# Dividing six PSUM banks between two kinds of work: three for the gates' products in place of two

## The reference, cut to what matters

```
p = h @ w_in;  xr, gate = split(p, [1536])          # 1536 = 12 heads x 128
xc = causal_depthwise_conv(xr, conv_w, conv_b)      # 4 taps
r = sigmoid(xh[head] @ w_rg[head] + b_rg)           # the gates' products: one 128x128
i = sigmoid(xh[head] @ w_ig[head] + b_ig)           # matrix per head and gate
a = exp(-8 * r * softplus(-lam))
hs = scan(a, sqrt(1 - a*a) * (i * xc))              # along time
y = hs * silu(gate)
h = h + y @ w_out
```

## Time and profile before

| | |
|---|---|
| median of 3 runs | 1717.25 us |
| the profiled execution's own time | 1717.2 us |
| its span, first to last instruction | 1715.1 us |
| PE busy | 1691.4 us, 99% |
| DVE, ACT, POOL busy | 871.1, 763.2, 967.1 us |
| mean granted TensorE clock | 0.999 |

### The profile page before, as it was taken

The page is one execution under the profiler, slowest core; times in us unless marked ns, Lnnn a source line. Parts: engine busy times, 40 slices in busy tenths (PEclk is TensorE's granted clock), DMA queues, the critical chain, the costliest instruction groups (busy, mean ns, idle before and its releaser), DMA issues.

```text
span 1715.1 us, 20931 instructions
## 1 busy us (share of the span) xinstructions
PE 1691.4 (99%) x8044; PEld 1396.4 (81%) x8044; DVE 871.1 (51%) x1251; ACT 763.2 (44%) x1203; POOL 967.1 (56%) x606
## 2 busy tenths in 40 slices
PE   9999999999999999999999999999999999999998
PEld 7888888777778997888888888888678888888887
DVE  4999997757787885522212121386644221212124
ACT  5223335377867763343222222454765332323234
POOL 5859655657678575654444444664547444444464
PEclk9999999999999999999999999999999999999999
DMA  5322323222245233222222222222112222222221
GB/s 177 100 97 87 123 98 112 98 73 87 86 183 201 68 124 130 99 96 92 95 98 98 99 98 99 86 98 99 50 48 89 98 99 98 99 92 94 97 99 62
DMA packets 56258, 172.65 MB, mean 101 GB/s; under 512 B 6496, under 2 KB 14816, under 8 KB 55264
## 3 DMA queue, kind: packets, MB, share of 16 engines
q1 hardware_dynamic: 56160, 171.33, 28.9%
HBM read 165.01 MB, written 6.29 MB: 100 GB/s over the span
## 4 chain that ended last, share of the span: by engine, by line
PE 70%; DVE 5%; ACT 3%; issue 2%; POOL 1%; DMA 1%; SPq 0%; DVEq 0%; ACTq 0%
PE B L319 57%; PE B L1712 1%; PE B L2464 1%; PE B L2466 1%; PE B L2462 1%; PE B L2260 1%; PE B L2360 1%; PE B L2339 1%; DVE SW L1175 1%; PE B L302 1%; DVE B L1041 1%; PE B L1639 1%; PE B L1604 1%; PE B L304 1%; PE B L303 1%
## 5 line engine op out<-in xcount | busy, mean ns | idle before, releaser
L295 POOL TENSOR_TENSOR WL<-RAW,WH 128x1024 fp32r<-128x1024 f32 x280 | 679.0, 2427 | 618.3 <-ACT WH L291 618.0
L291 ACT ACTIVATE WH<-RAW 128x1024 fp32r<-128x1024 f32 x281 | 296.8, 1058 | 634.3 <-PE B L319 600.2
L319 PE MATMUL B<-P0h,WH 128*128 128x512 f32 x1088 | 424.6, 390 | 2.0 <-DVE Yl L444 1.8
L319 PE MATMUL B<-P0l,WH 128*128 128x512 f32 x1088 | 418.0, 389 | 0.3 <-DVE P0l L448 0.3
L319 PE MATMUL B<-P0h,WL 128*128 128x512 f32 x1088 | 274.4, 389 | 0.0
L319 PEld LDWEIGHTS B<-P0h,WH 128*128 128x128 f32 x1088 | 204.3, 188 | 45.8 <-DVE Yl L444 2.6
L319 PEld LDWEIGHTS B<-P0l,WH 128*128 128x128 f32 x1088 | 204.3, 188 | 42.8 <-DVE P0l L448 0.8
L319 PEld LDWEIGHTS B<-P0h,WL 128*128 128x128 f32 x1088 | 204.2, 188 | 42.4
L455 DVE TENSOR_TENSOR H<-H,B 128x512 f32<-128x512 f32 x88 | 60.2, 686 | 288.2 <-PE B L319 288.1
L1992 DVE SCALAR_TENSOR_TENSOR TMP<-B,RS 128x512 f32<-128x512 f32 x64 | 44.1, 691 | 258.5 <-PE B L319 244.1
L319 PE MATMUL B<-P1h,WH 128*128 128x512 f32 x448 | 174.7, 390 | 0.0
(11 more groups left out here) (362 smaller groups left out, 2686.5 us busy)
## 6 DMA issues: line engine op xcount, KB each, us to landing
RAW<-in_w SPq DMA_DIRECT2D x281, 512.0 KB, 3.2
PX<-in_zeros SPq DMA_DIRECT2D x4, 1024.0 KB, 9.4
H<-in_xT SPq DMA_DIRECT2D x8, 256.0 KB, 5.4
U<-u SPq DMA_DIRECT2D x32, 64.0 KB, 2.0
g<-GB SPq DMA_DIRECT2D x8, 256.0 KB, 2.2
GB<-g SPq DMA_DIRECT2D x32, 64.0 KB, 2.0
out<-Q SPq DMA_DIRECT2D x4, 512.0 KB, 3.6
CA<-in_zeros SPq DMA_DIRECT2D x1, 1920.0 KB, 10.0
```

Source lines behind the costliest of these rows:

```text
L291: act.activation(WH[:, i % NS, :], RAW[:, i % NR, :], ACT.Copy).then_inc(*inc("w_hi", i))
L295: eng.tensor_tensor(WL[:, i % NS, :], RAW[:, i % NR, :], WH[:, i % NS, :].bitcast(F32), ALU.subtract).then_inc(*inc(lo_of(i), i))
L319: return pe.matmul(b[:, :], w[:, ws[c]], x[:, c, :], start=start, stop=stop)
```

## The change

One number: how many of the six banks go to `rbanks`. The gates' products go round in three banks in place of two; X and G go round in three in place of four. From O0 on all six are in one queue, as before.

```
     def pe_odd(pe):
-        for _ in range(2):
+        for _ in range(3):
             rbanks.queue.append(banks.queue.popleft())
```

## The result

The changed kernel takes 1737.41 us (median of 4 runs, 1736.43 to 1738.10) against 1717.61 (4 runs) before. The ratio is 1.0114, 95% interval 1.0103 to 1.0126: 19.8 us slower. The profiled execution took 1737.19 us, its span is 1735.1.

A forecast was written before the change was run, and what follows sets the result against it. TensorE, busy 99% of the span, was taken as the bound, so new waits are paid in full: 1717.2 + 11.95 (19.0 of new waits, less 2.1 swallowed and 4.95 won in rounds) + 2.2 for the clock = 1731.3 us, range 1727.5 to 1737.5.

The forecast's parts named there:

- The new waits: TensorE's units X3, X8, X10, G3, G9 and O2 wait for VectorE's low parts to free banks: 19.0 us in all.
- The rounds: Gates' products in R0, R1 and R2 lose less with three banks: 0.8, 3.1 and 1.05 us won, 4.95 in all.
- the forecast's own reason for R1: At R1 VectorE and ScalarE have caught up with a TensorE 6 us late, so stalls of 4.0 shrink to 0.9.
- faster rival: Only the gates' waits change, the banks' return does not bind: 4.95 us less, 1712.2 us; chance 0.04.
- Waits swallowed: Today's bank waits at X11 (0.6 us) and G10 (1.5 us) vanish behind the new waits: 2.1 us.
- The running delay: How much later TensorE is at a place than in the trace before; forecast 11.95 us after O2.
- The clock: One fall of TensorE's clock to half rate, in G9's 6.9 us wait: 2.2 us, the middle of none and 4.4.
- the three falls as a rival: The clock falls in all three long waits (X8, G3, G9), 2.2 us each: 1734 to 1736 us; chance 0.18.
- The rows at the span's end: Granted clock still 1.00 in the 5.2 us of TensorE's last four matmuls, 0.50 in the 1.8 us behind.
- X10's wait: X10 waits for X7's bank, 1.5 us; the three-falls rival let it swallow 1.5 us of the first fall.
- The range: 1727.5 to 1737.5 us: from 1729.1 less 1.6 for the sum's small terms, up to three falls.
- D: TensorE's running delay against the trace before; 11.9 us after O2, none of it given back to the kernel's end.

The follow-up runs named there:

- without the square root: The changed kernel with the recurrence's square root replaced by a second tanh, one table load of 1.28 us a round less: 1733.46 us, ratio 1.0091.
- The loss alone: Against the kernel before: X and G in three banks, gates' products still in two, sixth bank idle until O0: 1742.13 us, ratio 1.0146.
- The lent bank: The kernel before (two gates' banks, four for units), with the units' oldest bank lent to the gates for each round R: 1714.18 us, ratio 0.9982.
- the filled kernel: The changed kernel with 20, 16 and 29 matmuls on old data ahead of X8, G3 and G9, filling the long waits: 1732.90 us, ratio 1.0086.
- statistics' wait filled: The kernel before with one bank lent to the gates per round, plus four matmuls on old data between X0 and X1: 1713.96 us, ratio 0.9984.
- half filled: The changed kernel with 9, 7 and 14 matmuls on old data ahead of X8, G3 and G9: 1732.64 us, ratio 1.0092.

## Why the prediction was right, and where it was not

- **The new waits.** Forecast from start to start: X3 1.3, X8 4.9, X10 1.5, G3 3.8, G9 6.9, O2 0.6, sum 19.0. Measured: 1.3, 4.85, 1.6, 3.8, 6.9, 0.6, sum 19.0. The step that carried it, to ask of each low part what starts its chain and move it by that alone, was right at every place. The experiment without the square root shows it for X8 and G3. For G9 the same experiment shows its limit: the length of VectorE's table computations there is not fixed, and the forecast held because GpSimd's work lay beside them as before.
- **The rounds.** Forecast 4.95 us won, measured 23.7 - 18.1 = 5.6. The loss alone, set against the kernel before, shows that 2.0 of these come from TensorE's lateness at R1, as the forecast's own reason for R1 said. Its faster rival overlooked that: 1712.2 us counts R1's 3.1 us although TensorE would not be late there. The lent bank shows 3.1 us won in the rounds without lateness, and 1714.2 us. The seven waits of the earlier trace rows are not all that the rounds waited for banks: the 1.6 us of R1 stands under another entry (L302 <- DVE Yl L444: 1.8 us in 2), so the modelled tails are only a part of why the view shows less than the timeline. Waits swallowed: 2.1 both.
- **The running delay** without the clock's part at O3 is then 19.0 - 2.1 - 5.6 = 11.3 (and 0.2 for slower first matmuls behind waits), where 11.95 was forecast. In the filled kernel, where the first matmuls behind all six waits are slower and no unit is, it is 12.0.
- **The clock** is the term that was mis-sized: "I take the middle, 2.2 us, for one fall, in the 6.9 us wait". The size of a fall came out right (X8 2.4, G3 1.8, G9 2.3, from the units' lengths), their number did not. All three long waits brought one, 6.5 us (6.1 against the filled kernel's units), and the profiled execution had two more of 1.6 us each, in X1 and Q2. So the clock's term measured 9.7 us in that execution, where 2.2 was forecast: 7.5 us more. The rounds (0.6 more won) and the wait at L1728 (1.4, below) took a part of this back, and 5.7 us stand between the 14.1 forecast and the 19.8 measured. I had the three falls as a rival at 1734 to 1736 us and gave it 0.18. The rows at the span's end show a clock that stays up for 5.2 us with little work, but I read them as if the shorter waits were safe; they say nothing of another place. The size was luck in part. It is the middle between nothing and 4.4, and the earlier trace rows don't bound it from above: a matmul that is still slow at 8.89 says that the low level lasted at least until then.
- **X10's wait** did not swallow 1.5 us of the first fall, as that rival had it: it is 1.6 us in the changed kernel and 1.5 in the filled one. X7's low part comes behind the scaling of X8, which waits for X8's end, so a slower X8 moves the wait and doesn't fill it. The forecast had this dependence, and the rival left it out.
- **The range** held by 0.1 us, and that is luck. Its upper end was called three falls; the forecast's terms give 1735.7 for these, and the two more falls stood in no case.
- **What was given back.** I had D stay at its value to the end. In this trace some 21.4 us had come together behind Q2 (11.5, the clock's 9.7 and 0.2 from before X0), and 20.0 stood at the end. The wait at L1728 explains it, 2.4 us in the trace of before and 1.0 here. It is 0.9 to 2.3 in the other traces: 1.7 in the unchanged kernel's second one, 2.3 in the filled kernel, 0.9 in the lent one. So it doesn't go with the delay, and no run ties it to the change.

## What to carry to other kernels

Before a bank (or any buffer) is moved from one ring to another, list for each user of the smaller ring when its buffer came back and when the next one started, and add up what is short; ask what starts the chain that gives it back, since that tells by what it will move. When TensorE gets a new wait of well over 2 us, count a second price of about 2 us for the clock behind each, not behind the longest alone; with shorter ones it may come or not. And where two users are busy at different times, lend the buffer rather than divide it: here that turned 20 us of loss into 5 of gain.

## What the runs showed of the hardware

- The granted clock fell behind waits with 2.7, 3.3, 3.6, 4.7, 5.0 and 6.7 us of idle TensorE, and also behind 2.4 (G3 without the square root, whose unit took 1.6 us more than behind a wait at full clock). Shorter waits went both ways. It fell behind 2.1 us (filled, at 607) and 1.9 (statistics' wait filled, R1), and stayed up behind 2.1 (half filled, G3), 1.8 (lent, R1) and 1.6 (before, R1), one trace each. The price was 1.3 to 2.8 us a fall, by the unit behind it against the 5.57 us that it takes behind a wait at full clock.
- The clock falls by chance as well. Runs of the kernel before spread over 4.7 us in one group of 23 and 6.5 in another of 17, and the mean granted clock of a run goes with its time: in the group of 17 the kernel before took 1715.1 to 1716.3 us at 0.999 (5 runs), 1716.9 to 1718.0 at 0.998 (10) and 1720.0 and 1721.6 at 0.996.
- A VectorE operation on two tensors in SBUF (L1280 to L1283) takes 0.68 us alone and 1.6 to 2.9 beside operations of GpSimd (L295 and L1118). L444 or L1046, which have an operand in PSUM, keep their 0.69 beside them (at 489.74 and 486.91 in the changed kernel).
